# Where the operands of the split matmuls lie: chunks 2112 bytes apart, slots 4112, halves shifted by 32 and 128 bytes

## The chip, the core and the metric

The kernel runs on one core of a Trainium2 chip. Its engines are TensorE (PE: matmuls, with a row of its own, PEld, for the loads of the stationary operand), VectorE (DVE), ScalarE (ACT), GpSimd (POOL) and SyncE (SP), which issues most DMAs. SBUF has 128 partitions; an address below is a byte offset inside a partition, the same in all of them. The metric is the device time of one launch in microseconds (us).

## The reference

Three transformer-like layers act one after the other on `x` of 256 tokens by 1024 channels, all in float32. Cut to what matters:

```python
# layer 0: sliding-window attention and a state-space mixer, layer 1: stick-breaking attention
hn = rmsnorm(x, g); x = x + mixer(hn @ w_in) @ w_out
hn = rmsnorm(x, ffn_norm)
x = x + (silu(hn @ w_gate) * (hn @ w_up)) @ w_down          # 2816 wide, both layers
# layer 2: mLSTM and dilated attention, then a product-key expert layer
h2 = rms_norm(x, norm2_g)
q = h2 @ w_query                        # keys' scores, top 16 of each, top 16 of their sums
u = expert_u[idx]; a = gelu(h2 . u) * gate
x = x + a @ expert_v[idx]               # 16384 experts, 128 chosen for a token
```

The expert layer is computed densely: all 16384 rows of `expert_u` and `expert_v` are multiplied, and a matrix of gates, zero for experts that were not chosen, is put between the two products.

## The kernel before

**Strips.** All large weights are cut into 475 strips of 128 x 1024 float32 (512 KB), in the order of their use. A strip goes through one of three slots (`RING = 3`, strip n in slot n % 3) of three tensors: SP's DMA brings it to `ring`; ACT copies it to `w_hi` in type fp32r, which rounds it (`high`, L1425); DVE, in some stretches POOL, writes `w_lo = ring - w_hi` (`low`, L2037 and L3048), the rest that the rounding left. The activations are split in the same way: the input of a layer into `hT`, which holds for each of 8 chunks of 128 channels the 256 tokens' high part and then their low part, 2048 bytes for a chunk; the activations of the expert layer into `halves_hi` and `halves_lo`, where two tiles of 256 tokens take turns (the parities, `a_hi[:, e % 2, :]`).

**Products.** A product is the sum of high x high, low x high and high x low. TensorE runs them as:

- `strip_wide` (L651, L655): the expert layer's first product. For each chunk c one matmul with the 128 x 128 block c of `w_hi` as the stationary operand and the 512 columns of chunk c of `hT` (high and low part) as the moving one; then eight with `w_lo` and the 256 columns of the high part.
- `strip_fm`, `strip_two`, `strip_pair` (L600 to L680): the same by matmuls of 256 columns, for the projections and the feed-forward layers.
- `rows` (L795): 12 matmuls a strip, 128 tokens of `halves` (or `hT`) as the stationary operand, 512 columns of `w_hi` or `w_lo` as the moving one. It serves the second product of the expert layer and of the feed-forward layers and the outputs.
- `product` (L1375 to L1377): 7 pairs of the last product in a form with fewer products; `hT` is their stationary operand, by way of the view `tokens`.

TensorE waits for `high_ready` and `low_ready`; ACT's `high` waits for the strip and for `strip_done` of the strip three before; SP's next DMA into a slot waits for `low_ready`. Each engine runs its instructions in the order of the code. No scheduler is in between: the order is written by hand.

**Places.** Tensors of SBUF are placed one behind the other, in the order of the `sb(...)` calls, each start at a multiple of 32. The first free byte is 1152, and the kernel fills up to a round number:

```python
        sb("before_all", [P, (2048 - 1152) // 4])
        w_hi = sb("w_hi", [P, RING, D], F32R)
```

So `w_hi` starts at 2048, and every operand of the split matmuls starts at a multiple of 512 bytes. The view `r_x`, in the space of `arena`, takes the place of `hT` for the expert layer's queries.

Of the kernel before, what the change touches and what calls it, by code (L numbers as in the profile page):

```python
# [19 lines left out]
P = 128  # L20
D = 1024
T = 256
NT = T // P
KC = D // P
RING = 3
# [8 lines left out]
PH = 8  # L34
TOPK = 16
FREE_TILES = 78
NE1 = 128
HALF = NE1 // 2
OWN_LOWS = HALF + 2
PAIRS = 7  # L40
LEAD = 8
BETWEEN = 6
NV = NE1 - 2 * PAIRS
SHARED_LOWS = (33, 57)
# [6 lines left out]
F32R = mybir.dt.float32r  # L51
# [36 lines left out]
def strip_names():  # L88
# [23 lines left out]
    names += [("peer", "q", j) for j in range(2 * PH)]  # L112
    names += [("peer", "u", e) for e in range(NE1)] + [("peer", "v", n) for n in range(NV)]
    return names
# [43 lines left out]
def build(nc, A, out):  # L158
    with ExitStack() as ctx:
        def sb(name, shape, dt=F32):  # L160
            return ctx.enter_context(nc.sbuf_tensor(name, shape, dt))
# [2 lines left out]
            return ctx.enter_context(nc.semaphore(name))  # L164


        sb("before_all", [P, (2048 - 1152) // 4])
        w_hi = sb("w_hi", [P, RING, D], F32R)
        w_lo = sb("w_lo", [P, RING, D], F32R)
        ring = sb("ring", [P, RING, D])  # L170
        x_s = sb("x_s", [P, NT, D])
        xn = sb("xn", [P, NT, D])

        ARENA = NE1 * T
        with nc.sbuf_tensor("r_x", [P, KC, 2, T], F32R) as r_x:
# [1 line left out]
        with nc.sbuf_tensor("pair_r", [P, HALF * T], F32R) as pair_r:  # L177
            pass
        arena = sb("arena", [P, ARENA])
        hT = sb("hT", [P, KC, 2, T], F32R)  # L180
        hT_hi, hT_lo = hT[:, :, 0, :], hT[:, :, 1, :]

        halves_hi = sb("halves_hi", [P, 6 * P], F32R)
        halves_lo = sb("halves_lo", [P, 6 * P], F32R)
        a_hi, a_lo = (a[:, 0:2 * T].rearrange("p (a t) -> p a t", a=2) for a in (halves_hi, halves_lo))
        scale_diag = sb("scale_diag", [P, NT, P])
        scale_row = scale_diag[:, :, :].rearrange("p a b -> p (a b)")
        o_tri = sb("o_tri", [P, P], F32R)
# [135 lines left out]

        act = arena[:, 0:NE1 * T].rearrange("p (e t) -> p e t", t=T)
        L = Lay(FREE_TILES * T)
        keys_s = L(2, D)
# [18 lines left out]
        at = 2 * D  # L346
        blocks = pair_r[:, at:at + 4 * 7 * 512].rearrange("p (n h d) -> p n h d", n=2, h=2)
        b_hi, b_lo = blocks[:, :, 0, :], blocks[:, :, 1, :]
        tokens = hT[:, :, :, :].rearrange("p (n h c) s t -> p n h (c s t)", n=2, h=2)
        s_hi, s_lo = tokens[:, :, 0, :], tokens[:, :, 1, :]  # L350
        s_raw = arena[:, HALF * T:(HALF + 2) * T]
        t_raw = xn[:, :, :].rearrange("p a b -> p (a b)")
# [1056 lines left out]
        def _(sc):  # L1409
# [445 lines left out]
            def peer():  # L1855
# [68 lines left out]
                def wide_gelu(e, i=None):  # L1924

                    high(base + e + RING - 1, i)
                    if e > HALF or i is not None:
                        gelu_of(e - 1, i)
                    rest_out(e, i)
# [5 lines left out]
                with sc.Fori(1, HALF // UNROLL) as i:  # L1935
                    for e in range(HALF, HALF + UNROLL):
                        wide_gelu(e, i)
                for e in range(HALF + HALF // UNROLL * UNROLL, NE1 - 1):
                    wide_gelu(e)
# [1314 lines left out]
```

## Time and the profile before

| | |
|---|---|
| three runs | 1537.52, 1537.88, 1545.4 us; median 1537.88 us |
| profiled execution | 1545.27 us, of it a span of 1543.4 us from the first to the last instruction |
| mean granted clock of TensorE | 0.994 of full speed |
| PE, PEld busy | 99% and 85% of the span, 10088 matmuls with as many loads |
| DVE, ACT, POOL busy | 83%, 57%, 15% |
| DMA | 264.67 MB, 171 GB/s over the span |

A span is read from the first to the last instruction of the program. Busy times of a group of instructions are the union of their intervals, while the mean duration of one counts its whole way through the engine: matmuls overlap, so the time for which one holds the stream is the distance between the starts of two neighbours, and is read from pieces of the chain or of the timeline that hold many of them.

### The profile page before, as it was taken

How to read it: one execution, taken by the hardware profiler on the slowest of the kernel's cores; microseconds unless marked ns; L12 is line 12 of the kernel's file. 1: busy time of each engine (PE TensorE's matmuls, PEld its weight loads, DVE VectorE, ACT ScalarE, POOL GpSimd, SP SyncE). 2: the span in 40 equal slices, each digit the busy share in tenths (PEclk: the TensorE clock that was granted, in tenths of full speed). 3: DMA queues.
4: the chain of work that ended last, by engine and by line, in shares of the span. 5: the costliest groups of instructions: out<-in, count | busy, mean ns of one | idle time of the engine just before them, and what ended most of it. 6: DMA issues, size and time to landing. Idle time of an engine off the chain costs nothing.

```text
span 1543.4 us, 29887 instructions
## 1 busy us (share of the span) xinstructions
PE 1521.8 (99%) x10088; PEld 1318.6 (85%) x10088; DVE 1276.4 (83%) x2434; ACT 880.5 (57%) x1408; POOL 229.8 (15%) x99
## 2 busy tenths in 40 slices
PE   8999999999999999999999999999999999999999
PEld 8878888888888888998998888888888888878887
DVE  8878888755788888786789986899999999998886
ACT  7775434569754435765666666555554444456553
POOL 1001000125200001000678746200000000000000
PEclk9799999999999999999999999999999999999999
DMA  6135556553465555434445556555555555565563
GB/s 232 42 120 181 185 192 189 183 161 124 139 213 188 187 191 187 150 124 159 156 159 189 184 174 198 178 171 173 168 175 164 171 173 174 176 228 182 190 206 122
DMA packets 72501, 264.67 MB, mean 171 GB/s; under 512 B 8048, under 2 KB 8304, under 8 KB 72048
## 3 DMA queue, kind: packets, MB, share of 16 engines
q1 hardware_dynamic: 69696, 253.63, 50.1%
q10 hardware_dynamic: 2736, 10.11, 1.7%
q8 instruction: 45, 0.74, 0.2%
q14 instruction: 24, 0.20, 0.0%
HBM read 262.66 MB, written 1.05 MB: 171 GB/s over the span
## 4 chain that ended last, share of the span: by engine, by line
PE 86%; DVE 8%; ACT 3%; issue 2%; DMA 1%; DVEq 0%; ACTq 0%; SPq 0%
PE ps L795 31%; PE ps L651 21%; PE ps L655 11%; PE ps L619 3%; DVE arena L2037 3%; PE ps L620 3%; PE ps L623 3%; PE ps L1306 2%; PE ps L709 1%; DVE w_lo L2037 1%; PE ps L906 1%; DVE arena L2711 1%; DVE arena L2712 1%; PE ps L1375 1%; PE ps L1377 1%
## 5 line engine op out<-in xcount | busy, mean ns | idle before, releaser
L1425 ACT ACTIVATE w_hi<-ring 128x1024 fp32r<-128x1024 f32 x475 | 500.0, 1056 | 329.3 <-PE ps L795 179.3
L2037 DVE TENSOR_TENSOR w_lo<-ring,w_hi 128x1024 fp32r<-128x1024 f32 x383 | 466.0, 1218 | 56.5 <-ACT w_hi L1425 50.7
L651 PE MATMUL ps<-hT,w_hi 128*128 128x512 f32 x1696 | 427.1, 394 | 1.8 <-DVE arena L2037 0.9
L651 PEld LDWEIGHTS ps<-hT,w_hi 128*128 128x128 f32 x1696 | 307.1, 189 | 59.5 <-DVE arena L2037 1.6
L3048 POOL TENSOR_TENSOR w_lo<-ring,w_hi 128x1024 fp32r<-128x1024 f32 x92 | 224.7, 2450 | 747.0 <-DVE w_lo L2037 390.1
L795 PE MATMUL ps<-w_hi,halves_hi 128*128 128x512 f32 x632 | 250.3, 396 | 1.0 <-DVE halves_lo L2037 0.8
L795 PE MATMUL ps<-w_hi,halves_lo 128*128 128x512 f32 x632 | 247.0, 391 | 0.0
L655 PEld LDWEIGHTS ps<-hT,w_lo 128*128 128x128 f32 x1696 | 231.1, 190 | 17.4 <-DVE w_lo L2037 0.7
L655 PE MATMUL ps<-hT,w_lo 128*128 128x256 f32 x1696 | 236.6, 282 | 0.0
L795 PE MATMUL ps<-w_lo,halves_hi 128*128 128x512 f32 x632 | 170.4, 390 | 0.0
L2037 DVE TENSOR_TENSOR arena<-arena 128x256 f32<-128x256 f32 (+6 forms) x273 | 146.5, 550 | 14.5 <-ACT arena L1595 4.1
L795 PEld LDWEIGHTS ps<-w_hi,halves_hi 128*128 128x128 f32 x632 | 118.9, 188 | 26.3 <-issue 2.1
L795 PEld LDWEIGHTS ps<-w_lo,halves_hi 128*128 128x128 f32 x632 | 118.5, 188 | 25.8 <-DVE w_lo L2037 0.6
L795 PEld LDWEIGHTS ps<-w_hi,halves_lo 128*128 128x128 f32 x632 | 119.0, 188 | 22.3
L1897 ACT ACTIVATE xn<-ps 128x256 f32<-128x256 f32 x128 | 48.9, 382 | 111.8 <-PE ps L655 111.7
L2037 DVE TENSOR_TENSOR halves_lo<-arena,halves_hi 128x256 fp32r<-128x256 f32 (+1 forms) x166 | 74.3, 448 | 38.0 <-ACT halves_hi L1951 35.9
L2037 DVE TENSOR_TENSOR arena<-ps,scale_diag 128x512 f32<-128x512 f32 (+2 forms) x98 | 64.6, 659 | 41.2 <-PE ps L655 40.3
L619 PE MATMUL ps<-hT,w_hi 128*128 128x256 f32 x312 | 79.0, 291 | 0.0
L620 PE MATMUL ps<-hT,w_hi 128*128 128x256 f32 x312 | 77.1, 284 | 0.0
L1658 ACT ACTIVATE arena<-arena 128x256 f32<-128x256 f32 x44 | 18.4, 418 | 101.0 <-DVE arena L2037 101.0
L2037 DVE TENSOR_TENSOR arena<-ps,xn 128x256 f32<-128x256 f32 (+1 forms) x128 | 53.5, 418 | 20.4 <-ACT xn L1897 19.5
L1891 ACT ACTIVATE arena<-arena (+1 forms) x128 | 52.5, 410 | 29.0 <-DVE arena L2037 28.7
(378 smaller groups left out, 2001.4 us busy)
## 6 DMA issues: line engine op xcount, KB each, us to landing
ring<-in_strips SPq DMA_DIRECT2D x475, 512.0 KB, 3.5
arena<-in_pairs ACTq DMA_DIRECT2D x14, 512.0 KB, 5.0
const<-in_const SPq DMA_DIRECT2D x1, 1384.0 KB, 11.1
x_s<-in_x SPq DMA_DIRECT2D x2, 512.0 KB, 4.5
arena<-in_rel ACTq DMA_DIRECT2D x1, 1024.0 KB, 4.7
arena<-in_keys ACTq DMA_DIRECT2D x1, 1024.0 KB, 5.9
out<-x_s SPq DMA_DIRECT2D x4, 256.0 KB, 2.1
arena<-in_ssm_bc SPq DMA_DIRECT2D x1, 512.0 KB, 7.6
```

Source lines behind the costliest of these rows:

```text
L619: pe.matmul(out, w[0][:, cols], x[:, c, 0, :], start=c == 0, stop=False)
L620: pe.matmul(out, w[0][:, cols], x[:, c, 1, :], start=False, stop=False)
L623: mm = pe.matmul(out, w[1][:, c * P:(c + 1) * P], x[:, c, 0, :], start=False, stop=c == KC - 1)
L651: pe.matmul(bank, w[0][:, c * P:(c + 1) * P], hT[:, c].rearrange("p s t -> p (s t)"), start=c == 0, stop=False, skip_group_check=True)
L655: mm = pe.matmul(bank[:, 0:T], w[1][:, c * P:(c + 1) * P], hT_hi[:, c, :], start=False, stop=c == KC - 1, skip_group_check=True)
L795: return pe.matmul(ps[:, 2 * a + b, :], x[:, a * P:(a + 1) * P], w[part][:, b * 512:(b + 1) * 512], start=first and part == 0 and x is hi, ...
L1306: mm = pe.matmul(ps[:, 6 + g % 2, q * HALF:(q + 1) * HALF], oh_second[:, g % 3, q * P:(q + 1) * P], oh_gate[:, g % 3, (2 * q + part) * HAL ...
L1425: sc.activation(w_hi[:, n % RING, :], ring[:, n % RING, :], ACT.Copy).then_inc(high_ready, 1)
L1891: sc.activation(one(e, i), one(e, i), ACT.Gelu).then_inc(gelu_done, 1)
L1897: sc.activation(up_rest[e % 2], ps[:, up_bank(e), T:2 * T], ACT.Copy).then_inc(up_half, 1)
L2037: return ve.tensor_tensor(o, a, b, op)
L3048: po.tensor_tensor(w_lo[:, n % RING, :], ring[:, n % RING, :], w_hi[:, n % RING, :].bitcast(F32), ALU.subtract).then_inc(low_ready, 1)
```

## The change

Nothing is added to or taken from any engine's program: all five engines have the same instructions in the same order with the same waits. Only places in SBUF differ. (Four lines are added ahead of the engines' code, so that L651 is L655 in the kernel after, and so on; `hT` becomes a view of a tensor called `tokens_r`.)

```diff
+SLOT_GAP = 4
+CHUNK_GAP = 16
+PARITY_GAP = 8
...
-        sb("before_all", [P, (2048 - 1152) // 4])
-        w_hi = sb("w_hi", [P, RING, D], F32R)
-        w_lo = sb("w_lo", [P, RING, D], F32R)
+        w_hi, w_lo = (sb(name, [P, RING, D + SLOT_GAP], F32R)[:, :, 0:D] for name in ("w_hi", "w_lo"))
+        sb("behind_weights", [P, P - 2 * RING * SLOT_GAP])
...
-        hT = sb("hT", [P, KC, 2, T], F32R)
+        tokens_r = sb("tokens_r", [P, KC, 2 * T + CHUNK_GAP], F32R)
+        hT = tokens_r[:, :, 0:2 * T].rearrange("p c (s t) -> p c s t", s=2)
...
-        halves_hi = sb("halves_hi", [P, 6 * P], F32R)
+        halves_hi = sb("halves_hi", [P, 6 * P + 32], F32R)[:, 0:6 * P]
         halves_lo = sb("halves_lo", [P, 6 * P], F32R)
-        a_hi, a_lo = (a[:, 0:2 * T].rearrange("p (a t) -> p a t", a=2) for a in (halves_hi, halves_lo))
+        a_hi, a_lo = (a[:, 0:2 * (T + PARITY_GAP)].rearrange("p (a t) -> p a t", a=2)[:, :, 0:T]
+                      for a in (halves_hi, halves_lo))
...
-        tokens = hT[:, :, :, :].rearrange("p (n h c) s t -> p n h (c s t)", n=2, h=2)
+        tokens = tokens_r[:, :, :].rearrange("p (n h c) x -> p n h (c x)", n=2, h=2)[:, :, :, 0:8 * P]
```

The starts that follow from the sizes, in bytes, and what is left of them over multiples of 512:

| tensor | start before | over 512 | start after | over 512 | step after |
|---|---|---|---|---|---|
| `w_hi` | 2048 | 0 | 1152 | 128 | 4112 a slot |
| `w_lo` | 14336 | 0 | 13504 | 192 | 4112 a slot |
| `ring` | 26624 | 0 | 26272 | 160 | 4096 a slot |
| `x_s` | 38912 | 0 | 38560 | 160 | |
| `arena`, `r_x`, `pair_r` | 55296 | 0 | 54944 | 160 | |
| `hT` | 186368 | 0 | 186016 | 160 | 2112 a chunk |
| `halves_hi` | 202752 | 0 | 202912 | 160 | 1056 a parity |
| `halves_lo` | 205824 | 0 | 206112 | 288 | 1056 a parity |
| `const` | 210432 | 0 | 210720 | 288 | |

Inside an operand everything lies as before: the 512 columns of a chunk, the 1024 of a slot and the 256 tokens of a parity are contiguous.

## Rows read from the trace of the kernel before

**Rows 1.** The page: busy time of the engines, then the chain by engine.

```profile
PE 1521.8 (99%) x10088; PEld 1318.6 (85%) x10088; DVE 1276.4 (83%) x2434; ACT 880.5 (57%) x1408; POOL 229.8 (15%) x99
...
PE 86%; DVE 8%; ACT 3%; issue 2%; DMA 1%; DVEq 0%; ACTq 0%; SPq 0%
```

**Rows 2.** Groups by shape, TensorE: form, count | busy us, mean ns | idle before.

```profile
L651 PE MATMUL ps<-hT,w_hi 128*128 128x512 f32 x1696 | 427.1, 394 | 1.8 <-DVE arena L2037 0.9 <-ACT w_hi L1425 0.8
L795 PE MATMUL ps<-w_hi,halves_hi 128*128 128x512 f32 x632 | 250.3, 396 | 1.0 <-DVE halves_lo L2037 0.8
L655 PE MATMUL ps<-hT,w_lo 128*128 128x256 f32 x1696 | 236.6, 282 | 0.0
L619 PE MATMUL ps<-hT,w_hi 128*128 128x256 f32 x312 | 79.0, 291 | 0.0
L795 PE MATMUL ps<-w_hi,hT 128*128 128x512 f32 x192 | 49.7, 396 | 0.0
L619 PE MATMUL ps<-r_x,w_hi 128*128 128x256 f32 x112 | 28.5, 292 | 0.0
L1375 PE MATMUL ps<-pair_r,hT 128*128 128x512 f32 x49 | 19.3, 393 | 0.1
```

**Rows 3.** The chain in order of time: start us, us, what.

```profile
998.36 1.84 PE ps L651 x8
1000.20 0.95 PE ps L655 x8
1001.15 0.48 PE ps L1306 x16
...
1396.44 16.34 PE ps L795 x72
```

**Rows 4.** Timeline of TensorE: start us, us, what; two heads of the stick-breaking stage.

```profile
342.35 0.34 PE L1102 MATMUL ps<-halves_lo,o_tri 128*128 128x384 f32 x1
342.52 0.38 PE L1104 MATMUL ps<-arena,const 128*128 128x128 f32 x2
...
342.93 0.34 PE L1102 MATMUL ps<-halves_lo,o_tri 128*128 128x384 f32 x1
343.10 0.38 PE L1104 MATMUL ps<-arena,const 128*128 128x128 f32 x2
```

**Rows 5.** Groups by shape, loads of the stationary operand.

```profile
L1376 PEld LDWEIGHTS ps<-pair_r,hT 128*128 128x128 f32 x49 | 9.2, 188 | 1.9
...
L1104 PEld LDWEIGHTS ps<-arena,const 128*128 128x128 f32 x32 | 5.8, 188 | 0.0
```

**Rows 6.** Waits: who waited for whom: us in total, times, longest.

```profile
PE ps L651 <- ACT w_hi L1425: 0.8, 2, 0.5
...
ACT w_hi L1425 <- PE ps L795: 179.3, 112, 4.6
ACT w_hi L1425 <- DMA ring<-in_strips: 125.4, 80, 2.6
```

**Rows 7.** Groups by shape, DVE and ACT.

```profile
L2037 DVE TENSOR_TENSOR w_lo<-ring,w_hi 128x1024 fp32r<-128x1024 f32 x383 | 466.0, 1218 | 56.5 <-ACT w_hi L1425 50.7 <-POOL w_lo L3048 5.5
...
L2037 DVE TENSOR_TENSOR halves_lo<-arena,halves_hi 128x768 fp32r<-128x768 f32 x8 | 7.7, 956 | 0.2
...
L2037 DVE TENSOR_TENSOR arena<-ps,const 128x768 f32<-128x768 f32 x8 | 7.6, 956 | 9.7 <-PE ps L1104 9.6
...
L1425 ACT ACTIVATE w_hi<-ring 128x1024 fp32r<-128x1024 f32 x475 | 500.0, 1056 | 329.3 <-PE ps L795 179.3 <-DMA ring<-in_strips 125.4 <-PE ps L655 7.7
```

**Rows 8.** Stretches (us, busy by engine, clock, DMA share, GB/s), then DMA issues.

```profile
12.00:14.50 2.50, 2.50 (x19) 2.50 (x18) 2.15 (x15) 2.48 (x7) 0.00 (x0) 1.00 1.02 434
1187.00:1360.00 173.00, 173.00 (x1153) 139.74 (x1151) 163.52 (x347) 78.17 (x115) 0.00 (x0) 1.00 0.54 180
...
ring<-in_strips SPq DMA_DIRECT2D x475, 512.0 KB, 3.5
...
const<-in_const SPq DMA_DIRECT2D x1, 1384.0 KB, 11.1
```

## Prediction

> **What bounds the kernel now.** I read the page first. PE is busy for 1521.8 us of the span of 1543.4 us, and the chain that ended last is 86% PE [rows 1]. The list of waits then shows that TensorE hardly waits: the longest entry for the strips' matmuls on ACT's `w_hi` is 0.8 us in all, while ACT itself waits 179.3 us for PE and 125.4 us for strips to land [rows 6]. So the time is the sum of what TensorE's matmuls hold its stream for, and a change of places in SBUF counts only if it changes that, or if it makes something else late enough to stop TensorE.
>
> The mean of one matmul (394 ns for 512 columns [rows 2]) is no price, since matmuls overlap. The chain gives it: 72 matmuls of 512 columns take 16.34 us, 226.9 ns each; 8 of 256 columns take 0.95 us, 118.8 ns each; 16 of 64 columns in fp16 take 0.48 us, 30.0 ns each [rows 3]. The difference of the first two is 108.1 ns for 256 columns, 0.42 ns a column, which is the level of 2.4 GHz; the profile has the clock granted in full there [rows 8]. Taking the columns off at 2.4 GHz leaves a fixed part: 226.9 - 213.3 = 13.6 ns, 118.8 - 106.7 = 12.1 ns, and for fp16 30.0 - 26.7 = 3.3 ns. The split matmuls carry a fixed part four times that of the fp16 ones. This is the only part of TensorE's time that a place could plausibly touch, and I price it first.
>
> The large groups are 1696 + 3 x 632 + 192 + 3 x 49 = 3931 matmuls of 512 columns and 1696 + 3 x 312 + 3 x 112 = 2968 of 256 (L795, L619 and L1375 stand once for three groups of equal count) [rows 2]. Their fixed parts are 3931 x 13.6 ns + 2968 x 12.1 ns = 53.5 + 35.9 = 89.4 us. Above the fp16 level it is 3931 x 10.3 + 2968 x 8.8 ns = 66.6 us.
>
> **The change, part by part.** No instruction, wait or DMA is added, removed or moved on any engine, and no operand changes its length. What changes is where operands begin, so each part is a question of whether a beginning has a price.
>
> *Moving against stationary operand.* Before, both begin at multiples of 512 bytes, so a chunk being streamed and the next block being loaded always have the same place within 512. After, they differ in nearly all pairs (`hT` at 160 + 64 a chunk, `w_hi` at 128 + 16 a slot, `halves_hi` at 160 + 32 a parity). If the fixed part were a collision of these two reads, up to 89.4 us could go; if it belongs to the type, nothing does. For a collision speaks that all split matmuls have the fixed part and none was ever placed otherwise. Against it: it is the same 13 ns in matmuls of 512 and 256 columns, with `w`, `halves`, `hT` or `pair_r` on either side (the means of the 512-column groups agree within 3 ns [rows 2]), although the two places differ by any multiple of 512 from case to case; and the fp16 matmuls, whose operands also begin at round offsets, lack it. A fixed part that asks only for the type looks like the type's own. I take 0, with a gain of 66.6 us as the other end.
>
> The Trainium skill (TensorE: Matmul & The Clock Gate, "Back-to-back issue gap") gives N/2.4 + 2.5 ns for a matmul in a full-speed stream, 215.8 ns at 512 columns and 109.2 at 256. The trace disagrees for the split matmuls with 226.9 and 118.8; were the change to bring them to that rule, 3931 x 11.1 + 2968 x 9.6 ns = 72 us would go and the time be 1466 us, an estimate. The Trainium skill also has, on that page ("Step-by-step: what each phase is for", step 1), two independent read ports, one for the moving operand and one for the load, so that the load steals nothing from the running matmul; by that rule there is no collision to remove and the sum stays at 0. No row here separates the two.
>
> *Odd beginnings.* After, moving operands begin 16 or 32 bytes off a multiple of 64, and many cross multiples of 2048. A price for crossing is excluded by the cumulative sums of the stick-breaking stage: `o_sp_lo` of the even head lies from 1024 past a multiple of 2048 across the next, that of the odd head lies within one, and both hold the stream for 0.17 us [rows 4], 384/2.4 = 160 ns and the same 13 ns. A price for an odd beginning isn't excluded for moving operands. For stationary ones it is: `neg_ones` in `const` begins 4 bytes past a multiple of 16, and its load takes 188 ns like that of `hT` [rows 5]. I take 0 and keep, as the other end, 3.1 ns a matmul, by which the eight at 998.36 (1.84 us, 230 ns each) exceed those of 1396.44 [rows 3], the nearest row in which something disturbs the same matmul: (3931 + 2968) x 3.1 ns = 21.4 us.
>
> *DVE and ACT.* `w_lo` takes 1218 ns and `w_hi` 1056 ns a strip [rows 7]. A DVE subtraction of 768 columns takes 956 ns with its operands at round places, and an addition of the same size with a mask that begins 4 bytes past a multiple of 16 also 956 [rows 7]. I take 0. Were it 1%, `w_lo` would gain 12 ns a strip, which stands beside 2.7 us of matmuls.
>
> *DMA.* `ring` moves from a multiple of 512 to 160 past one. The large block of `const` lands at 4 past a multiple of 256 and runs at a share of 1.02 with 434 GB/s, 425 GB/s at full share, where strips make 180/0.54 = 333 [rows 8]. So an odd landing place isn't slower here. The Trainium skill (DMA: Bandwidth & Descriptors, "How a descriptor splits into AXI transactions") speaks against the change: a transfer that doesn't begin at a multiple of 256 bytes needs one transaction more, for a row of 4096 bytes 17 in place of 16, 6%, which on 3.5 us is 0.2 us a strip; the stretch with `const` shows nothing of the kind. Either way it is covered: in the expert layer's second product a strip is 12 x 226.9 ns = 2.72 us, a slot comes round after 8.17 us, and landing, high and low part take 3.5 + 1.06 + 1.22 = 5.78 us [rows 7, 8]. 2.4 us are left; if they were gone, each strip would wait for the excess.
>
> **The sum** is 0 + 0 + 0 + 0 us against the profiled execution's 1545.27 us. That execution lies 7.4 us above the median of the three runs, 1537.88 us, which two of the three meet; so I predict 1538 us.
>
> **The rivals.** *The fixed part is a collision, and the skew removes it.* All of it down to the fp16 level gives 1538 - 67 = 1471 us; half of it, if only some pairs come apart, 1505 us; a tenth 1531. It decides from 7.7 us, 1.1 ns a matmul, on. *An odd beginning costs the moving operand a little,* the other sign: at 3.1 ns on all matmuls 1559 us, on the third that reads slot 1 (16 off a multiple of 32) 7.1 us, 1545. It also decides from 1.1 ns a matmul. *The ring lands late* because of its odd place: with 2.4 us of cover the time stays at 1538; it would count only where a landing takes 5.9 us and not 3.5.
>
> **How the numbers follow.** A difference of 0.5%, 7.7 us, is about what a measurement of this kernel can tell from none. No change I give 0.52, since every row that compares places shows none. The collision gets 0.26: 0.11 for more than half of the fixed part, 0.15 for less. The odd beginnings get 0.20, and all other ways to be slower 0.02. A range from 1506 to 1556 us leaves out the larger collision (0.11) and the upper end of the odd beginnings (0.07). For the likeliest case alone it is 1531 to 1546 us. So faster 0.26, same 0.52, slower 0.22.
>
> **What will show it.** If I am right, the 72 matmuls between two `product` groups still take 16.3 us, the eight of L655 (then L659) 0.95 us, and the means of `w_lo`, `w_hi` and the strips' landing stay within 1%. A collision removed shows as less than 16.0 us for the 72; if the eight of 256 columns alone fall, it is a matter of `hT`'s chunks. Odd beginnings that cost show as more than 16.4 us, in a rhythm of three strips. I am wrong if the time leaves 1531 to 1546 while these pieces stay: then the change acts through waits, and ACT's or DVE's rows must have moved.

## The result and the profile after

The kernel after takes 1546.78 us in the median of 18 runs (1546.21 to 1554.14), the kernel before, on the same chip, 1539.23 us (1537.15 to 1545.89, 18 runs). The ratio is 1.005 with a 95% interval of 1.0037 to 1.0064: slower by 7.55 us, 0.5%, and the interval doesn't include 1. Some executions of either kernel (7 of 18 before, 3 of 18 after) end some 7 us later, among them that of the profile of before, whose trace has 17.1 us at a granted clock of 0.5, the level of 1.2 GHz, from 50.9 us on; the medians of the others are 1538.26 and 1546.69 us, 8.43 us apart, and pieces are compared below, not the two spans.

The page of the kernel after, busy time and then the chain by engine, answers to [rows 1]:

```profile
PE 1522.0 (99%) x10088; PEld 1306.5 (85%) x10088; DVE 1280.4 (83%) x2434; ACT 880.9 (57%) x1408; POOL 229.5 (15%) x99
...
PE 83%; DVE 11%; ACT 3%; issue 2%; DMA 0%; DVEq 0%; ACTq 0%
```

TensorE is still the bound and still busy for 99%. The waits of ACT and SP's transfers have hardly moved; the view of waits, then the groups by shape of DVE, ACT and the loads, then the DMA issues, all of the kernel after:

```profile
ACT w_hi L1429 <- PE ps L799: 188.6, 113, 4.8
ACT w_hi L1429 <- DMA ring<-in_strips: 121.9, 79, 2.7
...
L2041 DVE TENSOR_TENSOR w_lo<-ring,w_hi 128x1024 fp32r<-128x1024 f32 x383 | 466.0, 1218 | 56.1 <-ACT w_hi L1429 50.4 <-POOL w_lo L3052 5.5
L1429 ACT ACTIVATE w_hi<-ring 128x1024 fp32r<-128x1024 f32 x475 | 499.9, 1056 | 334.0 <-PE ps L799 188.6 <-DMA ring<-in_strips 121.9 <-PE ps L659 8.1
L1108 PEld LDWEIGHTS ps<-arena,const 128*128 128x128 f32 x32 | 5.8, 188 | 0.0
...
ring<-in_strips SPq DMA_DIRECT2D x475, 512.0 KB, 3.5
```

Against [rows 5 to 8] every duration is the same: 1218 and 1056 ns, 188 ns a load, 3.5 us to landing. What moved is the distance between matmuls. The chain of the kernel after in order of time (start us, us, what), at places that answer to [rows 3]:

```profile
999.02 0.94 PE ps L659 x8
999.97 1.85 PE ps L655 x8
1001.81 0.93 PE ps L659 x8
1002.74 0.48 PE ps L1310 x16
...
1395.09 16.73 PE ps L799 x72
```

The 72 matmuls of 512 columns took 16.34 us before, 226.9 ns each, and take 16.73 us now, 232.4 ns each. The eight of 256 columns go the other way, from 0.95 us to 0.93 or 0.94. The sixteen in fp16, which the change doesn't touch, stay at 0.48 us. The groups by shape of TensorE say the same; they answer to [rows 2]:

```profile
L655 PE MATMUL ps<-tokens_r,w_hi 128*128 128x512 f32 x1696 | 430.9, 396 | 2.0 <-DVE arena L2041 1.0 <-ACT w_hi L1429 0.9
L799 PE MATMUL ps<-w_hi,halves_hi 128*128 128x512 f32 x632 | 252.6, 400 | 0.8 <-DVE halves_lo L2041 0.7
L659 PE MATMUL ps<-tokens_r,w_lo 128*128 128x256 f32 x1696 | 234.3, 281 | 0.0
...
L623 PE MATMUL ps<-tokens_r,w_hi 128*128 128x256 f32 x312 | 77.2, 286 | 0.0
```

Groups of 512 columns hold the engine longer (427.1 to 430.9 and 250.3 to 252.6 us), groups of 256 columns shorter (236.6 to 234.3 and 79.0 to 77.2 us; of the last, 0.8 us belong to the stretch at 1.2 GHz, since e6 below, whose distances match those of before modulo 256, has 78.2). To add it up I took from the two traces the distance from the start of each split matmul to the start of the next matmul. The 4122 of 512 columns sum to 954.2 us before and 967.2 us after, +13.0 us or 3.2 ns each; the 3448 of 256 columns to 424.6 and 420.0 us, -4.6 us. Nine of the latter lie in before's stretch at 1.2 GHz. Four of them in the timeline of before (start us, us, what), 213 or 214 ns from start to start:

```profile
66.46 0.41 PE L619 MATMUL ps<-hT,w_hi 128*128 128x256 f32 x1
66.68 0.41 PE L620 MATMUL ps<-hT,w_hi 128*128 128x256 f32 x1
66.89 0.41 PE L619 MATMUL ps<-hT,w_hi 128*128 128x256 f32 x1
67.10 0.41 PE L620 MATMUL ps<-hT,w_hi 128*128 128x256 f32 x1
```

The nine take 2.08 us; the same nine take 1.18 us in e6. So 0.9 us of the 4.6 come from the clock, and 3.7 us, 1.1 ns each, from the places. Together that is +9.3 us, against 7.55 us between the medians and 8.43 us between those of the executions that don't end late; the sums are no better than that, since some 115 of the distances of 512 columns and 12 to 15 of those of 256 are over 260 ns and hold a wait. The distances of all other matmuls of TensorE sum to 153.4 us before, 146.1 us after, and 146.0 us in e6, whose trace has the full clock throughout; 245 of them lie in before's stretch. So the change of time is in the stream of the split matmuls, as two effects of opposite sign.

### The profile page after: what moved, and what is told of

Same layout as the page of the kernel before. It is cut to its first block, busy times and chain, and to the rows that moved or that the text cites. A ratio compares the mean times of both kernels' runs of the same rounds, so it can differ in the third digit from the quotient of the medians.

```text
span 1545.0 us, 29887 instructions
## 1 busy us (share of the span) xinstructions
PE 1522.0 (99%) x10088; PEld 1306.5 (85%) x10088; DVE 1280.4 (83%) x2434; ACT 880.9 (57%) x1408; POOL 229.5 (15%) x99
## 4 chain that ended last, share of the span: by engine, by line
PE 83%; DVE 11%; ACT 3%; issue 2%; DMA 0%; DVEq 0%; ACTq 0%
PE ps L799 32%; PE ps L655 21%; PE ps L659 11%; DVE arena L2041 4%; PE ps L1310 2%; PE ps L623 2%; PE ps L627 2%; PE ps L624 2%; PE ps L713 1%; DVE w_lo L2041 1%; PE ps L1380 1%; PE ps L1379 1%; PE ps L1381 1%; DVE arena L2715 1%; DVE arena L2716 1%
## 5 line engine op out<-in xcount | busy, mean ns | idle before, releaser
L1429 ACT ACTIVATE w_hi<-ring 128x1024 fp32r<-128x1024 f32 x475 | 499.9, 1056 | 334.0 <-PE ps L799 188.6
L2041 DVE TENSOR_TENSOR w_lo<-ring,w_hi 128x1024 fp32r<-128x1024 f32 x383 | 466.0, 1218 | 56.1 <-ACT w_hi L1429 50.4
L655 PE MATMUL ps<-tokens_r,w_hi 128*128 128x512 f32 x1696 | 430.9, 396 | 2.0 <-DVE arena L2041 1.0
L655 PEld LDWEIGHTS ps<-tokens_r,w_hi 128*128 128x128 f32 x1696 | 306.7, 188 | 62.3 <-DVE arena L2041 1.6
L799 PE MATMUL ps<-w_hi,halves_hi 128*128 128x512 f32 x632 | 252.6, 400 | 0.8 <-DVE halves_lo L2041 0.7
L659 PEld LDWEIGHTS ps<-tokens_r,w_lo 128*128 128x128 f32 x1696 | 228.9, 188 | 19.2 <-DVE w_lo L2041 0.7
L659 PE MATMUL ps<-tokens_r,w_lo 128*128 128x256 f32 x1696 | 234.3, 281 | 0.0
L799 PE MATMUL ps<-w_lo,halves_hi 128*128 128x512 f32 x632 | 173.7, 395 | 0.0
L2041 DVE TENSOR_TENSOR arena<-arena 128x256 f32<-128x256 f32 (+6 forms) x273 | 150.8, 566 | 8.7 <-ACT arena L1637 2.1
L623 PE MATMUL ps<-tokens_r,w_hi 128*128 128x256 f32 x312 | 77.2, 286 | 0.0
L624 PE MATMUL ps<-tokens_r,w_hi 128*128 128x256 f32 x312 | 75.4, 281 | 0.0
```

Source lines behind the costliest of these rows:

```text
L623: pe.matmul(out, w[0][:, cols], x[:, c, 0, :], start=c == 0, stop=False)
L624: pe.matmul(out, w[0][:, cols], x[:, c, 1, :], start=False, stop=False)
L655: pe.matmul(bank, w[0][:, c * P:(c + 1) * P], hT[:, c].rearrange("p s t -> p (s t)"), start=c == 0, stop=False, skip_group_check=True)
L659: mm = pe.matmul(bank[:, 0:T], w[1][:, c * P:(c + 1) * P], hT_hi[:, c, :], start=False, stop=c == KC - 1, skip_group_check=True)
L799: return pe.matmul(ps[:, 2 * a + b, :], x[:, a * P:(a + 1) * P], w[part][:, b * 512:(b + 1) * 512], start=first and part == 0 and x is hi, ...
L1429: sc.activation(w_hi[:, n % RING, :], ring[:, n % RING, :], ACT.Copy).then_inc(high_ready, 1)
```

## The experiments

Two theories stood after the result. *Distance:* what counts is how far the place that TensorE streams from lies from the place that the next block is loaded from, taken modulo some power of two; before, it was a multiple of 512 everywhere. *Odd beginnings:* a moving operand that begins off a multiple of 64 costs by itself, as my rival had it. The table holds all runs; "512" and "256" are the sums over the starts as above, each less that of the kernel before (954.2 and 424.6 us; the latter has the 0.9 us of the clock in it, as have those of e1 and e3, so the column "256" reads 0.9 us too low in all other rows), and "72" is the piece of the chain with 72 matmuls of 512 columns. The medians with an interval are those of 4 executions for e2 and e4, of 9 to 18 for the others.

| kernel | what differs, in bytes | us (before on that chip) | difference | ratio, 95% | 72 | 512 | 256 |
|---|---|---|---|---|---|---|---|
| after | all | 1546.78 (1539.23) | +7.55 | 1.0037 to 1.0064 | 16.73 | +13.0 | -4.6 |
| e1 | every start 160 on | 1538.93 (1538.18) | +0.75 | 0.9979 to 1.0012 | 16.34 | +0.6 | -0.2 |
| e2 | slots 4112 | 1545.14 (1538.18) | +6.96 | 1.0038 to 1.0086 | 16.65 | +9.0 | -2.8 |
| e3 | chunks 2112 | 1540.95 (1538.18) | +2.77 | 1.0006 to 1.0034 | 16.35 | +7.2 | -3.3 |
| e4 | halves 1056, low part 128 on | 1545.64 (1538.18) | +7.46 | 1.0032 to 1.0065 | 16.75 | +8.0 | +0.5 |
| e5 | slots 4160 | 1542.50 (1538.35) | +4.15 | 1.0008 to 1.0048 | 16.65 | +8.8 | -3.4 |
| e6 | slots 4352 | 1538.54 (1538.35) | +0.19 | 0.9977 to 1.0019 | 16.35 | +0.2 | +0.4 |
| e7 | slots 4100 | 1543.83 (1538.35) | +5.48 | 1.0015 to 1.0061 | 16.78 | +11.8 | -5.0 |
| e8 | 64 on, for 256 columns alone | 1534.66 (1538.51) | -3.85 | 0.9958 to 0.9989 | 16.34 | -0.2 | -5.8 |
| e9 | slots 4192, parities 1072 | 1545.62 (1538.51) | +7.11 | one run | 16.75 | +11.5 | -3.9 |
| e10 | e8, low parts 32, 128, 192 | 1538.30 (1537.70) | +0.60 | one run | 16.34 | +0.5 | -5.2 |
| e11 | e8, low parts 16, 96, 224 | 1535.46 (1537.70) | -2.24 | one run | 16.34 | +2.0 | -4.7 |

**e1_all_160: every start 160 on, all steps as before.** All distances between operands stay; all beginnings become odd.

```diff
-        sb("before_all", [P, (2048 - 1152) // 4])
+        sb("before_all", [P, (2048 - 1152 + 160) // 4])
```

> Every tensor of the split matmuls is moved by the same 160 bytes; steps stay 4096, 2048 and 1024. Theory 'pairs' (a matmul's stream slows when the place of its moving operand against that of the block being loaded changes from matmul to matmul): no pair changes, so 1538 to 1541 us and 226.9 ns a matmul of 512 columns in the value stage. Theory 'odd beginnings' (a moving operand that begins off a multiple of 512 costs): all of the loss or more, 1546 us, and 230 ns or more.

No change. The chain of this kernel:

```profile
1397.16 16.34 PE ps L795 x72
```

A beginning 160 past a multiple of 512 (32 past one of 64) costs nothing, for the matmuls or for `ring`, which now also lies there. As the cause of the loss odd beginnings are refuted. A start 16 past a multiple of 32 with all distances kept wasn't run, but e2 and e4 slow matmuls whose moving operand stays where it was.

**e2_slots: the slots alone 4112 apart.** `w_lo` and `ring` are kept at multiples of 512, so only slots 1 and 2 lie 16 and 32 bytes off everything else.

```diff
+        w_hi, w_lo = (sb(name, [P, RING * (D + 4) + 116], F32R)[:, 0:RING * (D + 4)].rearrange(
+            "p (r d) -> p r d", r=RING)[:, :, 0:D] for name in ("w_hi", "w_lo"))
```

> Only the slots' step of 4112. Inside a strip the pairs keep their place. Theory 'pairs': within 2 us of before. Theory 'odd beginnings': two slots of three make the 1896 matmuls of the value rows begin odd, 3.3 ns each on two thirds, +4 us, to be seen in a rhythm of three strips.

It costs 7 us alone. The chain of this kernel in the expert layer's first product, strip after strip:

```profile
894.82 1.82 PE ps L651 x8
896.64 0.95 PE ps L655 x8
897.59 1.87 PE ps L651 x8
899.46 0.95 PE ps L655 x8
900.42 1.87 PE ps L651 x8
902.28 0.93 PE ps L655 x8
903.22 1.82 PE ps L651 x8
```

Here is a rhythm of three: the strip in slot 0, at distance 0, takes 1.82 us, those at 16 and 32 take 1.87. The moving operand of these matmuls, `hT`, lies where it did. In slots 1 and 2 the distance is constant from matmul to matmul, and it costs all the same. A form of the theory in which the distance must change between neighbours falls with it: a constant distance that isn't a multiple is enough.

**e3_chunks: the chunks of `hT` alone 2112 apart.**

```diff
+        tokens_r = sb("tokens_r", [P, KC, 2 * T + 16], F32R)
+        hT = tokens_r[:, :, 0:2 * T].rearrange("p c (s t) -> p c s t", s=2)
```

> Only the chunks' step of 2112. Both theories see the 1696 wide matmuls slow by 3.3 ns (+5.6 us) and some 3000 of 256 columns gain 1.5 ns (-4.5 us): within 2 us of before. The rows with halves stay at 226.9 ns in both.

Only the products with `hT` differ: the wide matmuls of the first product go from a mean of 229.4 to 232.4 ns, its low ones from 119.1 to 117.5 ns (from the starts), so that almost half of the loss is given back (+7.2 and -3.3 us). The 72 matmuls, which read `halves`, stay at 16.35 us.

**e4_halves: the halves alone, parities 1056 apart and the low part 128 on.** This moves stationary operands only.

```diff
+        halves_hi = sb("halves_hi", [P, 6 * P + 32], F32R)[:, 0:6 * P]
...
+        sb("behind_halves", [P, 96])
+        a_hi, a_lo = (a[:, 0:2 * (T + 8)].rearrange("p (a t) -> p a t", a=2)[:, :, 0:T]
+                      for a in (halves_hi, halves_lo))
```

> Only the halves: parities 1056 bytes apart, the low part 128 bytes off the high one. They are stationary operands alone. Theory 'pairs': the place changes by 128 between the matmul with the high and that with the low part, 1896 x 3.3 ns = +6.3 us, and 230 to 233 ns in the value stage. Theory 'odd beginnings': 0 us, 226.9 ns, since the moving operands begin where they did.

It costs 7.5 us, though no moving operand of the strips' products has left its place. The chain of this kernel, then the loads of the moved operand:

```profile
1394.92 16.75 PE ps L797 x72
...
L797 PEld LDWEIGHTS ps<-w_hi,halves_lo 128*128 128x128 f32 x632 | 119.0, 188 | 23.8
```

Only the loaded operand has moved; its loads take 188 ns as before, and it is the matmuls that follow each other more slowly. So it is the pair that counts. It also shows that the parts don't add: 7.0 (e2), 2.8 (e3) and 7.5 us (e4) alone, 7.55 us together. In the rows with `halves` alone, e2 adds 5.2 us to the sum over the starts, e4 8.3 us, and both together, in the kernel after, 7.5 us: a pair that is off already pays no more for more skew.

**e5_slots_64: slots 4160 apart, distances 0, 64 and 128.** Is 64 or 128 the period?

```diff
+        w_hi, w_lo = (sb(name, [P, RING * (D + 16) + 80], F32R)[:, 0:RING * (D + 16)].rearrange(
+            "p (r d) -> p r d", r=RING)[:, :, 0:D] for name in ("w_hi", "w_lo"))
```

> Slots 4160 bytes apart, so slots 0, 1 and 2 lie 0, 64 and 128 bytes from a round distance to the other operand; nothing else moves. Theory 'distance with a period of 512' (a pair settles at 226.9 ns only when the distance between the beginnings of the moving operand and of the block being loaded is a multiple of 512): strips of slot 0 settle at 227 ns, those of slots 1 and 2 stay at 230 to 235 ns, 1545 us. Theory 'distance with a period of 64' (four lines of 16 bytes): all three settle, 1539 us.

Neither. The chain of this kernel:

```profile
894.60 1.84 PE ps L651 x8
896.44 0.95 PE ps L655 x8
897.39 1.87 PE ps L651 x8
899.26 0.91 PE ps L655 x8
900.18 1.85 PE ps L651 x8
902.03 0.95 PE ps L655 x8
```

The strip at 64 takes 1.87 us for its wide matmuls, but its low ones take 0.91 us: 113.7 ns each, against 120 at distance 0. So the loss at 512 columns and the gain at 256 come from the same distance.

**e6_slots_256: slots 4352 apart, distances 0, 256 and 512.**

```diff
+        w_hi, w_lo = (bass.AP(t.tensor, t.offset, [list(t.ap[0]), [D + 64, RING], [1, D]])
+                      for t in (sb(name, [P, RING * D + 128], F32R)[:, :] for name in ("w_hi", "w_lo")))
```

> Slots 4352 bytes apart, distances 0, 256 and 512. Period of 512: slots 0 and 2 settle at 227 ns, slot 1 doesn't, about a third to a half of the loss, 1541 to 1542 us. Period of 256 or less: all three settle, 1539 us.

Like the kernel before in every piece:

```profile
1390.05 16.35 PE ps L795 x72
```

With 64 and 128 off and 256 and 512 like 0, the period, among powers of two, is 256 bytes.

**e7_slots_4: slots 4100 apart, distances 0, 4 and 8.** One element off is the smallest step there is.

```diff
+        w_hi, w_lo = (sb(name, [P, RING * (D + 1) + 125], F32R)[:, 0:RING * (D + 1)].rearrange(
+            "p (r d) -> p r d", r=RING)[:, :, 0:D] for name in ("w_hi", "w_lo"))
```

> Slots 4100 bytes apart, distances 0, 4 and 8. If lines of 16 bytes are what two reads meet in, 4 and 8 bytes still share the line for most columns and slots 1 and 2 settle near 227 ns, 1539 to 1541 us; if the distance must be an exact multiple, they stay at 230 to 235 ns, 1545 us.

Four bytes are enough, and worst:

```profile
1413.56 16.78 PE ps L795 x72
```

By the starts, matmuls at distance 4 follow each other after some 238 ns, at 8 after some 232, at 0 after 227 once settled. Distance 0 is a narrow good place for 512 columns, not the end of a slope.

**e8_by_kind: each kind of matmul at its own distance.** If 512 columns want 0 and 256 columns something else, blocks that are loaded for matmuls of 256 columns are put 64 bytes on in their slot, and all other steps stay multiples of 256.

```diff
+def shift(strip, low):
+    layer, part, c = strip
+    wide = layer.startswith("mlp") and part in ("gate", "up") and c > 0 or strip[:2] == ("peer", "u")
+    narrow = part in ("gate", "up", "q", "k", "qa", "ka", "if", "z", "u") or strip[:2] == ("even", "v")
+    return (16 if low else 0 if wide else 16) if wide or narrow else 0
...
+def slot(tensor, n, low):
+    at = shift(STRIPS[n], low)
+    return tensor[:, n % RING, at:at + D]
...
-                return w_hi[:, n % RING, :], w_lo[:, n % RING, :], n, i
+                return slot(w_hi, n, False), slot(w_lo, n, True), n, i
```

> Every step is a multiple of 256, and the parts of strips that are loaded for matmuls of 256 columns (all of a strip of a projection, the low part of a wide strip) lie 64 bytes on in their slot, so that the moving operand begins 64 bytes before the loaded block; all matmuls of 512 columns keep a distance of a multiple of 256. Theory 'distance': a stream of 256 columns settles at 113.7 ns, as in slot 1 of the run with steps of 4160, in place of 120: some 3200 matmuls x 5 to 6 ns = 16 to 19 us faster, 1519 to 1523 us, with 226.9 ns for 512 columns in the value stage unchanged. Rival: what settled there needed the wide half of the strip at the same distance, and eight matmuls after a change of distance don't settle: under 5 us.

At 1534.66 us it is faster than both kernels, by 3.85 us (0.26%) than the one before. The chain of this kernel, then groups by shape and waits of TensorE:

```profile
894.19 0.94 PE ps L669 x8
895.13 1.84 PE ps L665 x8
...
1388.13 16.34 PE ps L809 x72
...
L669 PE MATMUL ps<-hT,w_lo 128*128 128x256 f32 x1696 | 234.6, 281 | 0.0
L633 PE MATMUL ps<-r_x,w_hi 128*128 128x256 f32 x112 | 27.4, 288 | 0.0
...
PE ps L665 <- DVE arena L2051: 2.8, 3, 1.7
PE ps L1101 <- DVE arena L2443: 1.6, 5, 0.3
```

The wide matmuls are as before. The expected 16 to 19 us didn't come; the gain is the rival's "under 5 us". Long rows of 256 columns, such as the queries from `r_x`, come down from 120 to 113 ns (medians of the starts; the group from 28.5 us [rows 2] to 27.4). The eight low ones behind eight wide ones come only to 117.8 ns, 0.94 us, although the distance is the same 64. So the distance isn't all; what ran before it counts too. Part of the gain comes back as waits. Of the sum for 256 columns, the distances under 260 ns fall by 9.1 us (416.3 to 407.2, with the nine at 1.2 GHz counted as in e6), while the 15 longer ones, which hold a wait, take 11.6 us where 11 took 7.4 before. The list of waits names DVE's `arena`: 2.8 us at L665 where it was 0.9 before (at L651), and 1.6 us at L1101 where the kernel before had none to list. Of the 2 us between -6.0 us of the sums and -3.85 us of the medians, 0.9 us are the clock's; the rest I didn't trace further.

**e9_scan_96_48: slots 4192 and parities 1072 apart,** to see several further distances in one run.

```diff
+        w_hi, w_lo = (sb(name, [P, RING * (D + 24) + 56], F32R)[:, 0:RING * (D + 24)].rearrange(
+            "p (r d) -> p r d", r=RING)[:, :, 0:D] for name in ("w_hi", "w_lo"))
...
+        a_hi, a_lo = (a[:, 0:2 * (T + 12)].rearrange("p (a t) -> p a t", a=2)[:, :, 0:T]
+                      for a in (halves_hi, halves_lo))
```

> Slots 96 bytes and parities 48 bytes off, for distances not yet seen: 0, 48, 96, 144, 192, 208 between moving and loaded operand in the value stage, 64 and 160 for the wide matmuls. Theory 'distance with a period of 256, best at 0': no strip settles below 226.7 ns, all but the one at 0 lie at 229 to 238. Rival: some distance is better than 0 for 512 columns, under 226.

No distance brings 512 columns to settle under 227 ns; by the starts only matmuls at 0 settle there. The others average 229 to 234 ns by slot. The smallest loss is that of the wide matmuls with the loaded block 192 on (slot 2): 226, 229 and 232 ns in turn, 229.4 on average, as much as eight at distance 0 take with their settling.

**e10_lows and e11_lows2: as e8, with the low parts of the wide strips elsewhere,** at 32, 128, 192 (e10) and 16, 96, 224 (e11) by slot. Is there a distance at which the eight low ones also reach 113 ns?

```diff
+def shift(strip, low, n, lows=(8, 32, 48)):
...
+    return (lows[n % RING] if low and wide else 0 if wide else 16) if wide or narrow else 0
```

> As the kernel by kind, but the low parts of wide strips lie 32, 128 or 192 bytes on (slots 0, 1, 2) in place of 64. Theory 'distance': what a run of eight matmuls of 256 columns settles at after the wide half is set by its distance; some of the three comes under the 0.94 us that 64 bytes gave, at best 0.91 us. Rival: after the wide half at distance 0 no distance gets under 0.94 us, since the first matmuls decide it.

> The same with 16, 96 and 224 bytes. Theory 'distance': one of the six under 0.93 us for the eight, which on 212 wide strips would be worth 2 to 6 us. Rival: all six between 0.94 and 0.96 us.

No. The chain of e10, then of e11:

```profile
895.42 0.95 PE ps L669 x8
...
898.20 0.96 PE ps L669 x8
...
901.00 0.94 PE ps L669 x8
```

```profile
895.01 0.95 PE ps L669 x8
...
897.81 0.94 PE ps L669 x8
...
900.57 0.95 PE ps L669 x8
```

All six lie at 0.94 to 0.96 us, none near the 0.91 that e5 has behind wide matmuls at distance 64. The means of the low ones are 118.7 (e10) and 118.0 ns (e11) against 117.8 in e8. One execution each doesn't rank e10 and e11 against e8.

The queries from `r_x` lie in e10 and e11 as they do in e8, 64 off, and there they take 118 ns, not 113 (medians of the starts; so do those of e5's slot 1, also 64 off). The group of e10, then that of e11, where e8 has 27.4 us and 288 ns:

```profile
L633 PE MATMUL ps<-r_x,w_hi 128*128 128x256 f32 x112 | 28.2, 291 | 0.0
L633 PE MATMUL ps<-r_x,w_hi 128*128 128x256 f32 x112 | 28.2, 291 | 0.0
```

In e8 this stream also begins at 118 ns and falls to 113 within its first 48 matmuls. So 113 and 118 are two levels at one distance, in long rows as behind wide matmuls, and part of e8's gain is a level that the distance alone doesn't give.

## Why the prediction was right in its range and off by 0.5%

The time, 1546.78 us, lies in the range of 1506 to 1556; the forecast of no change at 1538 us is off by 8.8 us, and the likeliest case's own range, 1531 to 1546, just misses it. That the wide range holds the time is luck: its upper end was drawn for the odd beginnings, which e1 refutes, and the term that moved stood at 0 with a gain as its only other end. The 7.7 us by which the chances were divided was too coarse as well: the interval of this result is 0.27% wide, and that of e8, at -0.26%, doesn't include 1 either.

**The step that failed** is "Moving against stationary operand", at "I take 0, with a gain of 66.6 us as the other end". The argument was that the fixed part is the same wherever the two places "differ by any multiple of 512". That is true, and it is one case: all multiples of 512 are distance 0 modulo 256, so those rows compared nothing (e6 against e2, e5 and e7). They couldn't tell whether the fixed part is the type's own or depends on the places. The second fault is the bound. From a fixed part I concluded that a change of distance could only take some of it away; the runs show that distance 0 is the best place for 512 columns, and that leaving it costs 3.2 ns a matmul, 13.0 us over 4122 matmuls. For 256 columns the guess of a gain was right in sign: 1.1 ns in the kernel after, 6 to 7 ns at best, of the 12.1 priced. (The sum priced 3931 and 2968 of the 4122 and 3448 matmuls; and [rows 8] has the clock for other stretches than the pieces of [rows 3], but the trace has it in full from 68 us on, so the price of a column stands.)

**"Odd beginnings"** had the other sign and nearly the size: 3.1 ns a matmul on all, 1559 us, where 512 columns show 3.2 and 256 columns -1.1. Its cause is refuted by e1 (+0.75 us, interval across zero), and its sign that I had named, a rhythm of three strips, is missing in the kernel after: the rows with `halves` average 232.4, 232.3 and 232.6 ns in the three slots, and the wide pieces take 1.85 or 1.86 us in one strip like the other, since the chunks' distances vary within each. That its size fitted has a reason: the row that I took it from, the eight at 998.36 [rows 3], is nearly the same thing. Even at distance 0 the stream runs at 224 to 236 ns for some ten matmuls after an interruption before it settles at 227. In the kernel before, the first strip of the expert layer's second product behind the sixteen fp16 matmuls goes, after a first gap of 312 ns, 229, 233, 236, 224, 231, 236, 228, 232, 231, 227, 227 ns (from the starts, medians), and the eight at 998.36, behind eight of 256 columns, go 234, 236, 228, 232, 231, 227, 227, 226. At other distances the runs show no such settling.

**What held:** the order of the bounds (PE 99%), no price for crossing a multiple of 2048 (in e1 every chunk of `hT` crosses one; the matmuls of [rows 4] take 174 to 177 ns with either head), 0 for DVE and ACT (1218 and 1056 ns), 0 for DMA: `ring` lies 160 past a multiple of 256 now and still lands in 3.5 us. The prediction took one more transaction for this from the Trainium skill (DMA: Bandwidth & Descriptors, "How a descriptor splits into AXI transactions"); that section tells of bytes that are fetched in vain below an odd start, and here the side that is written moved, so no run here tests it. For an odd stationary beginning only half held: a common shift costs nothing (e1), but the 188 ns of a load [rows 5] could not exclude a price, since e4's loads take 188 ns too and its matmuls lose 5.7 ns each.

**The two rules on TensorE.** The Trainium skill (TensorE: Matmul & The Clock Gate, "Step-by-step: what each phase is for", step 1) has independent ports for the moving operand and for the load, which is to steal nothing; I weighed it as speaking for 0. e4 speaks against it here: moving only the loaded operand takes the 72 matmuls from 16.34 to 16.75 us. The "Back-to-back issue gap" of the Trainium skill, N/2.4 + 2.5 ns, which that section calls the gap of an isolated matmul and the prediction that of a stream, is reached at no distance tried: 227 ns at 512 columns where it has 215.8, 113 at 256 where it has 109.2.

**What stays open.** That the two reads collide in the memory is an argument, not shown: the runs show that the pair of places counts, not where it does. No run takes away what the other engines and the DMAs read and write in SBUF; that they play a part is unlikely, since the sequences repeat to 1 ns (two strips in e2's slot 2 both go 237, 235, 232, 235, 232, 235, 231, 235). Which of the two stationary blocks counts, the one in use or the one being loaded, wasn't told apart: in the strips of the first product they lie a multiple of 512 from each other, and in e4's rows, where high and low part lie 128 apart, both orders are slow (medians of 235 ns with the high part in use and the low one next, 231 or 232 the other way). Why 256 columns gain where 512 lose, what chooses between 113 and 118 ns at the same distance of 64, and where the remaining 13.4 ns at 512 columns come from (226.7 settled, less 213.3), is open too. One reading narrows the last: at 1.2 GHz the matmuls of 256 columns shown above follow each other after 213 or 214 ns, and 256/1.2 is 213.3, so at that clock nothing is left of the fixed part. In e3, whose `hT` has its chunks 2112 apart, the same matmuls run in such a stretch too and take 213 or 214 ns: there the places don't show.

## What to carry to other kernels

In a kernel that is bound by a dense stream of split fp32 matmuls, let the moving operand and the blocks loaded beside it begin at the same place modulo 256 bytes for 512 columns, and try 64 bytes off for long runs of 256 columns, which gave 113 ns in one kernel and 118 in others, in place of 120; a common shift of all tensors by 160 bytes didn't matter. Rows that all share one case (here a multiple of 512) can't price the other cases, and a fixed part that looks like overhead may already be the best of them, so bound such a change on both sides. A gain on the bounding engine comes back in part as waits (9.1 us off e8's stream of 256 columns, 3.85 us off its time).

## What the runs showed of the hardware that I had not expected

- Split matmuls of 512 columns settle at 227 ns only where moving and loaded operand begin at the same place modulo 256 bytes; with the slots 4, 8, 16, 32, 64, 96, 128 and 192 off they average 229 to 238 ns.
- Matmuls of 256 columns have it the other way: 120 ns at the same place, 113 to 118 ns off it, with two levels at the same distance of 64 (113 and 118, each in long runs and behind wide ones).
- The stream has a memory: at distance 0 some ten matmuls of 512 columns pass after an interruption until it settles.
- The fixed part of 13 ns that split matmuls of 256 columns have at 2.4 GHz (120 ns) is gone at 1.2 GHz (213 or 214 ns).
- The loss doesn't add up: three parts that cost 7.0, 2.8 and 7.5 us alone cost 7.55 us together.
